# Two transformer models on one core: the norms between single-stream linears, with gain and root in one VectorE operation and more of the norm on GpSimd

## The reference

```python
def layer_norm(x, g, b):
    xf = x.astype(jnp.float32)
    mu = jnp.mean(xf, axis=-1, keepdims=True)
    var = jnp.mean(jnp.square(xf - mu), axis=-1, keepdims=True)
    return ((xf - mu) * lax.rsqrt(var + LN_EPS) * g + b).astype(x.dtype)

def modulate(x, shift, scale):
    return x * (1.0 + scale) + shift

h = modulate(x, mod[:, 0, 0], mod[:, 0, 1])
y = swiglu_ffn(h, ffn1_w_in[l], ffn1_w_out[l])
x = layer_norm(ALPHA * x + 0.5 * mod[:, 0, 2] * y, ln_g[l, 0], ln_b[l, 0])
h = modulate(x, mod[:, 1, 0], mod[:, 1, 1])
proj = h @ mix_w_in[l]
```

## Time and profile before

| | |
|---|---|
| runs | 3718.88, 3719.49 and 3723.9 us, median 3719.49 |
| the profiled execution's own time | 3719.87 us |
| its span, first to last instruction | 3718.1 us |
| mean granted clock of PE | 0.994 |
| PE, DVE, ACT, POOL busy | 3643.9, 2263.1, 1711.7, 727.0 us |

### The profile page before, as it was taken

One profiled execution on the slowest core, in us unless ns is written; L12 is line 12 of the kernel. 1 busy time (PEld: TensorE's weight loads), 2 busy tenths in 40 slices (PEclk: granted clock), 3 DMA queues, 4 the chain that ended last, 5 costly groups with the idle time before them and its releaser, 6 DMA issues.

```text
span 3718.1 us, 48896 instructions
## 1 busy us (share of the span) xinstructions
PE 3643.9 (98%) x19410; PEld 3076.8 (83%) x19410; DVE 2263.1 (61%) x2742; ACT 1711.7 (46%) x2648; POOL 727.0 (20%) x750
## 2 busy tenths in 40 slices
PE   8999999999999999999999999999999999999998
PEld 6888877888888888788888689888888888988886
DVE  5555766744574567777545488685655467875345
ACT  4444434543454454446433269454544244853223
POOL 2000302300120012032003437550000143642001
PEclk9999999999999999999999999999999999999999
...
DMA packets 71650, 417.37 MB, mean 112 GB/s; under 512 B 8976, under 2 KB 12176, under 8 KB 30480
## 3 DMA queue, kind: packets, MB, share of 16 engines
...
## 4 chain that ended last, share of the span: by engine, by line
PE 88%; DVE 7%; ACT 2%; issue 2%; POOL 1%; DMA 0%; DVEq 0%; SPq 0%; ACTq 0%; POOLq 0%
PE ps L2195 26%; PE ps L2196 25%; PE ps L2197 25%; PE ps L2933 2%; PE ps L2976 2%; DVE x_lat L3403 1%; DVE x_lat L3414 1%; DVE rstd_lat L3391 1%; PE ps L2911 1%; PE ps L2912 1%; DVE w_lo L3072 1%; PE ps L2670 1%; DVE x_lat L3347 0%; DVE h_lo L3424 0%; PE ps L2946 0%
## 5 line engine op out<-in xcount | busy, mean ns | idle before, releaser
L2195 PE MATMUL ps<-h_hi,w_lo 128*128 128x512 f32 (+2 forms) x2872 | 1079.8, 376 | 24.4 <-DVE h_lo L3424 15.3
L2197 PE MATMUL ps<-h_hi,w_hi 128*128 128x512 f32 (+2 forms) x2872 | 1065.0, 371 | 0.0
L2196 PE MATMUL ps<-h_lo,w_hi 128*128 128x512 f32 (+1 forms) x2800 | 1039.3, 371 | 0.0
L3072 DVE TENSOR_TENSOR w_lo<-raw,w_hi 128x2048 fp32r<-128x2048 f32 (+3 forms) x251 | 533.3, 2125 | 654.9 <-ACT w_hi L1423 654.5
L1423 ACT ACTIVATE w_hi<-raw 128x2048 fp32r<-128x2048 f32 (+3 forms) x260 | 454.0, 1746 | 927.2 <-PE ps L2197 908.4
L2195 PEld LDWEIGHTS ps<-h_hi,w_lo 128*128 128x128 f32 (+1 forms) x2872 | 541.4, 188 | 134.3 <-DVE h_lo L3424 24.7
L2197 PEld LDWEIGHTS ps<-h_hi,w_hi 128*128 128x128 f32 (+1 forms) x2872 | 541.4, 189 | 94.3
L2196 PEld LDWEIGHTS ps<-h_lo,w_hi 128*128 128x128 f32 x2800 | 528.2, 189 | 87.8 <-issue 0.5
L2195 PE MATMUL ps<-hid_hi,w_lo 128*128 128x512 f32 (+1 forms) x1272 | 487.7, 383 | 3.9 <-DVE w_lo L3072 2.7
L2196 PE MATMUL ps<-hid_lo,w_hi 128*128 128x512 f32 (+1 forms) x1272 | 483.8, 380 | 0.0
L2197 PE MATMUL ps<-hid_hi,w_hi 128*128 128x512 f32 (+1 forms) x1272 | 483.4, 380 | 0.0
...
## 6 DMA issues: line engine op xcount, KB each, us to landing
...
```

The source lines that it names most:

```text
L2195: eng.matmul(out, lo_w, hi_x, start=first, stop=False, skip_group_check=True)
L2196: eng.matmul(out, hi_w, lo_x, start=False, stop=False, skip_group_check=True)
L2197: return eng.matmul(out, hi_w, hi_x, start=False, stop=last, skip_group_check=True)
L3072: eng.tensor_tensor(w_lo[:, slot, 0:ln.width], raw[:, slot, 0:ln.width], w_hi[:, slot, 0:ln.width].bitcast(F32), ALU.subtract).then_inc(s_ ...
```

## The change

It concerns the norms with `nm.singly` set. For these:

- DVE multiplies the centred x by the gain and by the reciprocal root in one operation per chunk, into sq_h_lat (`gained`), and leaves x alone. ACT rounds sq_h_lat plus the shift (`rounded`). DVE forms the remainder from sq_h_lat, the shift and the rounded value, per chunk (`split_chunk`). POOL and ACT no longer compute an unrounded h.
- POOL subtracts the mean for pairs 3 and 4 of the first part and pairs 2, 3, 4 of the second (`POOL_CENTRES`, counted as groups 0 to 4 in the code). For that ACT copies the mean from PSUM to SBUF (`mean_copied`).
- POOL takes the remainder of the first half of the second unit's weights.
- POOL multiplies x by the reciprocal root, pair by pair, in both parts (`scaled_x`), before its gain and bias.
- PE's fillers in the third group are 2 instead of 8, and it waits for h_lo chunk by chunk.

```diff
 ON_ACT = (3, 5, 7)
 BUSY = (1, 2, 8, 0, 0)
+BUSY_SINGLY = (1, 2, 2, 0, 0)
+POOL_CENTRES = ((3, 4), (2, 3, 4))
 FF2 = 4096
...
+            nm.singly = bool(nm.name and nm.next and len(nm.streams) == len(nm.next.streams) == 1)
...
+            def centred(norm, j, g):
+                part, (k0, k1) = norm.parts[j], GROUPS[g]
+                x = X[part.st][:, k0:k1, part.cs]
+                eng.wait_ge(s_m0c, w.m0c + len(norm.streams) + j + 1)
+                eng.wait_ge(s_cent, w.cent + 4 * len(norm.streams))
+                eng.wait_ge(s_evac, last_evac(norm, j) if k1 == DC else tile_evac(norm, DC - 2))
+                eng.tensor_tensor(x, x, m0[part.st][:, part.cs].unsqueeze(1).broadcast_to([P, k1 - k0, HALF]),
+                                  ALU.subtract).then_inc(s_a32, 1)
+            def scaled_x(norm, part, j):
+                x = X[part.st][:, 2 * j:2 * j + 2, part.cs]
+                eng.wait_ge(s_v, part.v0 + 2 * j + 2)
+                eng.tensor_tensor(x, x, rstd[part.st][:, part.cs].unsqueeze(1).broadcast_to([P, 2, HALF]), ALU.mult)\
+                   .then_inc(s_n32, 1)
+            def singly(norm):
+                first, second = norm.parts
+                ln = norm.next
+                slot, c = (ln.g0 + 1) % 2, weight_half(ln, 0)
+                for g in POOL_CENTRES[0]:
+                    centred(norm, 0, g)
+                eng.wait_ge(s_whi2, ln.halved)
+                eng.tensor_tensor(w_lo[:, slot, c], raw[:, slot, c], w_hi[:, slot, c].bitcast(F32), ALU.subtract)\
+                   .then_inc(s_wlo2, 1)
+                for g in POOL_CENTRES[1]:
+                    centred(norm, 1, g)
+                for part in norm.parts:
+                    for j in range(DC // 2):
+                        scaled_x(norm, part, j)
+                eng.wait_ge(s_vec, w.vec + 7 * len(norm.streams))
+                for part in norm.parts:
+                    x = X[part.st]
+                    _, _, g, b = affine(norm, part.st)
+                    for k in range(DC):
+                        eng.wait_ge(s_n32, part.n32 + k // 2 + 1)
+                        eng.tensor_scalar(x[:, k, part.cs], x[:, k, part.cs], g[:, k:k + 1], b[:, k:k + 1], ALU.mult,
+                                          ALU.add).then_inc(s_xa, 1)
...
+            def mean_copied(norm, j):
+                part = norm.parts[j]
+                eng.activation(m0[part.st][:, part.cs], sum_of(j), ACT.Copy).then_inc(s_m0c, 1)
+            def rounded(norm, part, k0, k1):
+                b = affine(norm, part.st)[1]
+                for k in range(k0, k1):
+                    eng.wait_ge(s_v, part.v0 + k + 1)
+                    eng.activation(H[part.st][0][:, k, part.cs], sq_h[part.st][:, k, part.cs], ACT.Identity,
+                                   bias=b[:, k:k + 1]).then_inc(s_nhi, 1)
+            def singly(norm):
+                first, second = norm.parts
+                eng.activation(eps_t[:, 3:4], eps_t[:, 0:1], ACT.Sqrt)
+                square_last(norm, 0)
+                mean_squared(norm, 0)
+                mean_copied(norm, 0)
+                deviation(norm, 0)
+                eng.wait_ge(s_vec, w.vec + 7 * len(norm.streams))
+                rounded(norm, first, 0, 4)
+                second_unit(norm.next, 0)
+                square_last(norm, 1)
+                rounded(norm, first, 4, 5)
+                mean_squared(norm, 1)
+                rounded(norm, first, 5, 6)
+                mean_copied(norm, 1)
+                rounded(norm, first, 6, 7)
+                deviation(norm, 1)
+                rounded(norm, first, 7, DC)
+                second_unit(norm.next, 1)
+                rounded(norm, second, 0, DC)
...
-                            if k in [g[0] for g in GROUPS]:
-                                if n == 0 and not before_it:
-                                    busy(BUSY[GROUP_OF[k]])
-                                eng.wait_ge(s_nlo, len(GROUPS) * p.idx + GROUP_OF[k] + 1)
+                            if n == 0 and not before_it and k in [g[0] for g in GROUPS]:
+                                busy((BUSY_SINGLY if norm.singly else BUSY)[GROUP_OF[k]])
+                            if p in norm.parts and norm.singly:
+                                eng.wait_ge(s_nlo, p.lo0 + k + 1)
+                            elif k in [g[0] for g in GROUPS]:
+                                eng.wait_ge(s_nlo, p.lo0 + GROUP_OF[k] + 1)
...
+            def gained(norm, j, k):
+                part, g = norm.parts[j], GROUP_OF[k]
+                eng.wait_ge(s_rstd, 2 * part.nidx + 2)
+                if g in POOL_CENTRES[j]:
+                    eng.wait_ge(s_a32, part.a32 + POOL_CENTRES[j].index(g) + 1)
+                else:
+                    eng.wait_ge(s_u, part.u0 + g + 1)
+                eng.scalar_tensor_tensor(sq_h[part.st][:, k, part.cs], X[part.st][:, k, part.cs],
+                                         affine(norm, part.st)[0][:, k:k + 1], rstd[part.st][:, part.cs], ALU.mult,
+                                         ALU.mult).then_inc(s_v, 1)
+            def split_chunk(norm, j, k):
+                part = norm.parts[j]
+                hi, lo = H[part.st]
+                eng.wait_ge(s_nhi, DC * part.idx + k + 1)
+                eng.wait_ge(s_v, part.v0 + k + 1)
+                eng.scalar_tensor_tensor(lo[:, k, part.cs], sq_h[part.st][:, k, part.cs],
+                                         affine(norm, part.st)[1][:, k:k + 1], hi[:, k, part.cs].bitcast(F32), ALU.add,
+                                         ALU.subtract).then_inc(s_nlo, 1)
+            def singly(ln, norm):
+                last_tile(ln, 0)
+                if quarters_done(ln, 6) < 4:
+                    split_quarters(norm.next, quarters_done(ln, 6), 4)
+                deviation(norm, 0)
+                centred(norm, 0, 0)
+                centred(norm, 0, 1)
+                inverse(norm, 0)
+                eng.wait_ge(s_vec, w.vec + 7 * len(norm.streams))
+                for j in range(2):
+                    gained(norm, j, 0)
+                    gained(norm, j, 1)
+                    if j == 0:
+                        centred(norm, 0, 2)
+                    for k in range(2, DC + 2):
+                        split_chunk(norm, j, k - 2)
+                        if j == 0 and k == 5:
+                            last_tile(ln, 1)
+                        if j == 0 and k == DC:
+                            deviation(norm, 1)
+                        if k < DC:
+                            gained(norm, j, k)
+                    if j == 0:
+                        centred(norm, 1, 0)
+                        centred(norm, 1, 1)
+                        inverse(norm, 1)
+                        second_unit_half(norm.next)
+                eng.wait_ge(s_n32, norm.parts[1].n32 + DC // 2)
```

89 lines of the change are left out of this document (48 added, 41 removed).

## The result

The changed kernel takes 3761.5 us (median of 4 runs, 3759.7 to 3765.0) against 3719.2 us before (4 runs beside them): ratio 1.011, 95% interval 1.0098 to 1.0122. It is 42 us slower. The forecast was 3730 us, with a range of 3712 to 3744 us: the sign was right, the size was not, and the time is outside the range. It lies nearest to rival C (3753 us), which had a chance of 0.09.

A forecast was written before the change was run, and what follows sets the result against it. The prediction took PE, busy for 98% of the span, to bound the kernel. Per norm 1.3 + 0.5 + 0.5 - 0.6 = +1.7 us, for six norms +10 us on 3719.9: 3730 us, range 3712 to 3744.

The forecast's parts named there:

- rival C: POOL gets in after every DVE operation; four more remainders and gains wait: +33 us, 3753 us; chance 0.09.
- What bounds the kernel, and the first chunks: PE bounds the kernel; in chunks 0 to 3 of the first part the change wins 1.0 us per norm.
- The half of the weights: POOL's half of w_lo holds up remainder 4; the 1.0 us won is gone, and 0.1 with it.
- Chunks 5 to 7: Second deviation, root and POOL's centrings delay chunk 7 and the second unit: cost 0.8 to 1.8 us per norm, taken 1.3.
- Blocks between 414 and 416: In the first part POOL can get in once more ahead of DVE: up to 1.0 us per norm, taken 0.5.
- DVE's half of the weights: It follows remainder 7 and may reach PE's second unit late: 0 to 0.8 us per norm, taken 0.5.
- Second part: PE comes later than DVE, blocks by the scalings fall into slack, and a wait of 0.6 us per norm goes.
- DVE's last wait: After the norm, DVE's new wait for POOL's eighth scaling of x: 0, at most 1 us.
- The sign: The whole kernel gets slower: +10 us; slower by over 0.2% had a chance of 0.51.
- The sum: Per norm +1.7 us, ends +0.2 and +3.0; over six norms +10 us, +1 to +18.

The follow-up runs named there:

- e12_only_half: e6_all_dev with the first half of the second unit's w_lo put back on POOL: 3719.9 us.
- e5_dev: Changed kernel with the second part's deviation on DVE behind remainder 7 and its root on ACT behind rounding 7, as before the change: 3756.2 us.
- e4_all: Changed kernel with the edits of e1_half, e7_centres and e2_late together: 3719.6 us.
- e6_all_dev: e4_all with the edit of e5_dev too: 3713.1 us.
- e13_only_centres: e6_all_dev with POOL again centring pairs 2, 3 and 4 of the second part: 3734.3 us.
- e15_ptr: Changed kernel without DVE's last wait, POOL's new operations written as tensor-scalars with scalars read from SBUF, parts of the computation left out: 3719.0 us.
- e2_late: Changed kernel with POOL scaling x only behind DVE's last gain, and without DVE's last wait for the scalings: 3750.6 us.
- e14_only_scalings: e6_all_dev with POOL's scalings of x starting again as soon as both gains of a pair are done: 3735.9 us.
- e11_tt: Changed kernel without DVE's last wait for the eighth scaling of x, POOL's tensor-tensors kept: 3759.3 us.
- e3_fill: Changed kernel with filler products of PE, 8, 12, 12 and 8, in front of chunks 4 to 7 of the first part: 3758.3 us.
- e7_centres: Changed kernel with DVE, instead of POOL, centring the second part from PSUM: 3751.0 us.
- e1_half: Changed kernel with DVE again computing the first half of the second unit's w_lo, in front of chunk 4's remainder: 3744.3 us.

## Why the prediction was wrong

**What bounds the kernel, and the first chunks:** right. PE's waits for h_lo are where the time went, and chunks 0 to 3 ran on the forecast's schedule.

**The half of the weights:** right. Remainder 4 took 2.01 us, forecast 1.5 to 2.0, and ended 12.5 us after the norm's start, forecast 12.4. (The sum left out the 0.1 us per norm that the text had for it.) Put back alone it costs 1.1 us per norm (e12_only_half), over a kernel in which DVE spends 1.22 us on it.

**Chunks 5 to 7:** right for the order, 0.9 to 1.1 us per norm (e5_dev; e4_all to e6_all_dev, 6.6 us). Wrong for the centrings beside it: one block at most in front of chunk 7 was forecast.

**Blocks between 414 and 416:** this step failed. It took 0.5 us, between 0 and 1.0, with the words "a DVE that never pauses isn't held up, and one that pauses is". In the changed kernel DVE never pauses between 414.98 and 420.7, and four of its operations in a row take 1.5 us, 1.0 us more each. The centrings alone cost 3.5 us per norm (e13_only_centres). The reading came from one row, the 3.63 us of a tensor-scalar with its scalars in SBUF. Of these, 2.15 us lie under the operation of DVE that was already running, so two others passed it over, not three. e15_ptr shows this form passed over, and the change issues none of it there. The kernel before had the other form too. In DVE's timeline, and in POOL's:

```profile
654.25 0.68 DVE L3362 TENSOR_TENSOR x_sum_lat<-x_lat 128x512 f32<-128x512 f32 x1
654.85 1.77 DVE L3081 TENSOR_TENSOR w_lo<-raw,w_hi 128x512 fp32r<-128x512 f32 x1
```

```profile
654.36 1.72 POOL L1148 TENSOR_TENSOR ssum_lat<-ssum_lat,sq_a_lat 128x512 f32<-128x512 f32 x1 [2.25 <-ACT sq_a_lat L1620]
```

DVE stands end to end at 654.85, and POOL's tensor-tensor, waiting since 654.36, gets in first. In the trace of before there are 15 such places with a waiting tensor-tensor of POOL and DVE end to end, and at all 15 POOL gets in. (Two short ones, of 128x8, neither wait nor hold DVE up.) I had read one kind of row and applied it to the other.

**DVE's half of the weights:** 0.5 us, between 0 and 0.8, was forecast; in the changed kernel PE has no wait there at any of the six norms, because its second unit itself starts so late.

**Second part:** "Blocks by the scaling of x fall into that slack" was the forecast, and for the second part it held: four operations are blocked at the first norm, and PE waits for none of them. What failed is the place of the scalings. One gets in at remainder 6 and one at remainder 7 of the first part, and these are most of what e2_late won (10.9 us, with up to 2.2 us for DVE's last wait). Alone the scalings cost 3.8 us per norm (e14_only_scalings). There they get in as early as the gain at 411.6, and PE's new waits are again in the first part, but for one of 0.4 us in the second.

**DVE's last wait:** at most 2.2 us in all by the medians of e11_tt and the changed kernel, whose runs overlap. The forecast had 0 to 1 us per norm.

**The clock:** the forecast had no term for it. Its fall costs 9.1 us over the six norms by the distances of e3_fill, 3.2 us by its time.

**The sign:** not luck. From the half (e12_only_half, 3719.9 us) and the order (6.6 us) alone I estimate 3726 us, slower than before, and both steps were right.

**The rivals:** C had the mechanism and the place right. It priced four more blocks at 0.95 us and stopped at 33 us; what it left out is the clock. That 33 and the clock's 9 make 42 is partly luck: C kept the 0.5 us for DVE's half of the weights, which cost nothing. The Trainium skill ("SBUF — State Buffer", § SBUF: two separate sides) has whoever starts first hold the shared ports and the other blocked fully. I let the 3.63 us row speak against it. For the tensor-tensors of this change the rule, taken literally, is what every blocked row shows (1.03 us more for 128x512).

**The sum:** 42 us. Undone one at a time, the half gives 17, the centrings 10, the scalings (with the last wait) 11 and the order 5; undone together 48. Put back one at a time, the first three cost 7, 21 and 23. Blocks don't add up, and they miss in both directions. The centrings and the scalings cost more alone than in company, for two reasons: where the centrings go, the scalings move up into their place (e7_centres), and the scalings alone have nothing in front of them in POOL's order and begin at 408.6 us (e14_only_scalings) instead of 419.0. The half costs less alone, because beside the centrings it also makes DVE late enough for two more of them to get in (e1_half).
